# Filler transposes ahead of a wait in the scan, and two ScalarE splits behind eight evacuations, in a two-layer decoder trunk

## The reference

```python
xr, xw, xk, xv, xa, xg = [xf + xx * mu[i] for i in range(6)]
r = xr @ wr;  k = xk @ wk;  v = xv @ wv
w_log = -softplus(-(w0 + tanh(xw @ w1) @ w2)) - 0.5
decay = exp(-exp(w_log))
a = sigmoid(a0 + (xa @ a1) @ a2)          # the "rate"
g = sigmoid(xg @ g1) @ g2                 # the gate
...
def step(S, inp):                         # over the 256 tokens, 16 heads of 64x64
    sa = einsum('bhij,bhj->bhi', S, -kk_t)
    S = S * w_t + sa[..., None] * (kk_t * a_t) + v_t[..., None] * k_t
    y = einsum('bhij,bhj->bhi', S, r_t)
```

## Time and profile before

| | us |
|---|---|
| three runs | 1564.68, 1568.73, 1569.08 |
| median of the runs | 1568.73 |
| the profiled execution | 1557.25 |
| its span | 1555.2 |
| TensorE busy | 1521.9 (98%) |
| VectorE busy | 1264.2 (81%) |
| ScalarE busy | 997.4 (64%) |

### The profile page before, as it was taken

How to read it: one execution, slowest core, us unless ns; L and a number is a source line. 1 busy time by engine, 2 the same in 40 slices (tenths; PEclk the granted TensorE clock), 3 DMA queues, 4 the chain that set the end, 5 groups by cost and what they waited for, 6 DMA issues and landing times.

```text
span 1555.2 us, 21510 instructions
## 1 busy us (share of the span) xinstructions
PE 1521.9 (98%) x7832; PEld 1257.1 (81%) x7832; DVE 1264.2 (81%) x1449; ACT 997.4 (64%) x1139; POOL 9.3 (1%) x10
## 2 busy tenths in 40 slices
PE   8999999899999999999999999999999999999997
PEld 5678888589889767888888888888888888888885
DVE  3456666866866259999999999999999999999997
ACT  2244444553422138887887887878888888887886
POOL 0000000000000010000000000000000000000000
PEclk9999999999999999999999999999999999999999
DMA  9779443024003649999999999999999999999970
GB/s 362 286 277 300 163 162 109 0 82 140 22 1 110 227 176 400 397 377 363 387 366 358 387 361 359 385 381 343 383 381 344 381 379 349 376 379 357 370 292 27
DMA packets 203269, 439.36 MB, mean 283 GB/s; under 512 B 7217, under 2 KB 44337, under 8 KB 203090
## 3 DMA queue, kind: packets, MB, share of 16 engines
q1 hardware_dynamic: 200434, 434.05, 76.4%
q10 hardware_dynamic: 2208, 2.50, 0.5%
q0 software_dynamic: 576, 2.10, 0.3%
HBM read 427.09 MB, written 11.53 MB: 282 GB/s over the span
## 4 chain that ended last, share of the span: by engine, by line
PE 94%; DVE 3%; ACT 1%; issue 1%; DMA 0%; DVEq 0%; ACTq 0%
PE psum L1494 19%; PE psum L1496 19%; PE psum L1495 19%; PE psum L567 6%; PE psum L2227 5%; PE psum L2229 3%; PE psum L2155 2%; PE psum L842 2%; PE psum L2200 2%; PE psum L1512 2%; PE psum L2211 1%; PE psum L2213 1%; PE psum L2212 1%; PE psum L738 1%; PE psum L728 1%; PE psum L643 1%
## 5 line engine op out<-in xcount | busy, mean ns | idle before, releaser
L1694 DVE TENSOR_TENSOR w_lo<-ring,w_hi 128x1024 fp32r<-128x1024 f32 x672 | 805.0, 1221 | 51.5 <-ACT w_hi L1598 11.4
L1598 ACT ACTIVATE w_hi<-ring 128x1024 fp32r<-128x1024 f32 x672 | 711.4, 1062 | 186.6 <-PE psum L1496 186.4
L1494 PE MATMUL psum<-w_hi,xg_split 128*128 128x512 f32 x896 | 353.5, 395 | 0.4 <-DVE xg_split L1788 0.4
L1496 PE MATMUL psum<-w_lo,xg_split 128*128 128x512 f32 x896 | 349.4, 390 | 0.0
L1495 PE MATMUL psum<-w_hi,xg_split 128*128 128x512 f32 x896 | 348.8, 389 | 0.0
L1496 PEld LDWEIGHTS psum<-w_lo,xg_split 128*128 128x128 f32 x896 | 168.2, 188 | 35.7
L1494 PEld LDWEIGHTS psum<-w_hi,xg_split 128*128 128x128 f32 x896 | 168.2, 188 | 34.1 <-DVE xg_split L1788 0.6
L1495 PEld LDWEIGHTS psum<-w_hi,xg_split 128*128 128x128 f32 x896 | 168.4, 188 | 33.6
L1494 PE MATMUL psum<-w_hi,ht_split 128*128 128x512 f32 x448 | 176.0, 393 | 1.7 <-DVE w_lo L1694 1.7
L1496 PE MATMUL psum<-w_lo,ht_split 128*128 128x512 f32 x448 | 174.5, 390 | 0.0
L1495 PE MATMUL psum<-w_hi,ht_split 128*128 128x512 f32 x448 | 174.3, 389 | 0.0
(11 more groups left out here) (332 smaller groups left out, 1558.4 us busy)
## 6 DMA issues: line engine op xcount, KB each, us to landing
ring<-o_moe_wg_dram SPq DMA_DIRECT2D x56, 2048.0 KB, 9.1
ring<-o_moe_wu_dram SPq DMA_DIRECT2D x56, 2048.0 KB, 9.2
ring<-o_moe_wd_dram SPq DMA_DIRECT2D x56, 2048.0 KB, 9.1
ring<-e_ffn_wg_dram SPq DMA_DIRECT2D x11, 1024.0 KB, 5.5
ring<-e_ffn_wu_dram SPq DMA_DIRECT2D x11, 1024.0 KB, 8.7
ring<-e_ffn_wd_dram SPq DMA_DIRECT2D x11, 1024.0 KB, 10.6
expert_rows<-work SPq DMA_DIRECT2D x1, 8192.0 KB, 29.4
ring<-e_w_in_dram SPq DMA_DIRECT2D x2, 2048.0 KB, 18.1
```

Of the source, the lines that this page charges most:

```text
L1494: nc.tensor.matmul(dst, x_hi, hi, start=first, stop=False)
L1496: return nc.tensor.matmul(dst, x_hi, lo, start=False, stop=last_)
L1598: nc.scalar.activation(w_hi[:, (4 * i + n) % 4, :], piece(i, n), ACT.Copy).then_inc(m_hi, 1)
L1694: V.tensor_tensor(w_lo[:, r, :], piece(i, n), w_hi[:, r, :].bitcast(F32), ALU.subtract).then_inc(m_lo, 1)
```

## The change

Two edits, both of order only. No instruction is added or taken away, and no wait is added or taken away.

```diff
-            pe.wait_ge(y_zero, 3)
             pe.wait_ge(a_ma, 16)
             for _ in range(22):
                 nc.tensor.transpose(psum[:, 2, 0:P], ident, ident)
+            pe.wait_ge(y_zero, 3)
```

```diff
                 i_.then_inc(o_act, 1)
-                if n == 7:
-                    hi_x(0)
-                    hi_w(2)
+            hi_x(0)
+            hi_w(2)
             hi_x(1)
             hi_w(3)
```

## The result

Five executions of the changed kernel took 1552.04 us in the median (1550.95 to 1559.89). Five of the kernel before on the same chip took 1564.68 us (1564.31 to 1569.08). The ratio is 0.9916, with a 95% interval of 0.989 to 0.9942: 12.6 us less, where 5.8 were forecast. (Some 4 us of the distance to 1562.9 is only that these five runs of before have a median of 1564.68, the first three one of 1568.73.)

A forecast was written before the change was run, and what follows sets the result against it. TensorE's work and the gaps in it were taken to bound the kernel; 4.8 us (fillers) + 1.0 us (splits) = 5.8 us off the profiled 1557.25, ratio 0.9963, so 1568.73 became 1562.9 us, range 1557.5 to 1569.

The forecast's parts named there:

- the sum: Whole kernel: 4.8 + 1.0 = 5.8 us off the profiled 1557.25, giving 1551.45; same ratio 0.9963 on the median, 1562.9.
- part 2: Time mixing, two splits moved behind the rate's evacuations: TensorE's 1.00 us wait before the gate's first product goes, gaining 1.0 us.
- The bounds I gave: For the moved splits: at best the 1.0 us gap, at worst -1.0 us if lo_x(0)'s 2.0 us delay came through.
- Part 1's term: Scan, 22 fillers run inside the memset wait instead of behind it: L719 starts 4.75 us earlier; 4.8 us taken, bounds 4.2 to 5.0.
- The wait left: Sign in the scan: TensorE's 3.78 us wait shrinks to about 1.1 us and stands at L719.
- L1238 has lost its idle time: Sign in the scan: VectorE's first mask, L1238, no longer has 4.30 us of idle time before it, but none.
- Rivals A: Scan: the clock falls in the gap left ahead of L719; gain only 3.3 us, time 1565.4; chance 0.10.
- D: Scan from 433 on: clock falls behind the early fillers and isn't brought back; slower, 1574.9 us; chance 0.05.
- Rivals B: Time mixing: the moved splits gain nothing, another wait takes the gap's place; gain 4.8 us, time 1563.9; chance 0.07.
- C: Expert stage: ends where it did because the weight stream sets its pace; no gain, 1568.7 us; chance 0.11.
- TensorE's wait for L938 is gone: Sign at the gate's first product: this wait disappears and L592 starts 1.0 us earlier, at about 317.8.

The follow-up runs named there:

- the copy: The kernel before, run again unchanged: 1568.05 us in the median, ratio 1.0003; its profiled execution took 1568.47 us.
- part 2 alone: Kernel before with only hi_x(0) and hi_w(2) moved behind the rate's eight evacuations, the wait ahead of the fillers as before: 1556.68 us, ratio 0.9953.
- part 1 alone: Kernel before with only the wait for the memsets moved behind the 22 fillers, the splits where they were: 1566.23 us, ratio 0.9993.
- experiment 9: Part 1 alone plus 6 more transposes in the router's last two gaps (four ahead of its last rows, 12 for 10 behind): 1560.25 us, ratio 0.9969.
- experiments 5: Kernel before, orders kept, with 9 filler transposes behind the last rate product, in TensorE's 1.0 us gap: 1558.01 us, ratio 0.9947.

## Why the prediction was wrong

**The step that failed** is in the sum: "The runs' median is 11.48 us above the profiled execution. I take the same ratio for it: 1568.73 x 0.9963 = 1562.9." It took the profiled execution for a typical one, shorter only by chance. The runs show that it belongs to a group of 7 in 89. In its profile the clock does not fall at 309; in the copy's it does, and the missing 11 us stand right behind the very gap that part 2 closes. I had the 11.48 us in the text and explained it with nothing. Nearly twice the whole forecast, it called for a cause before a ratio.

**Part 2's term was mis-sized by that.** Its own gap is worth 1.08 us in the profiles and 0.8 us between free executions (forecast 1.0). What it mostly prevents is worth far more: free executions go from 7 of 89 (4 of 40 on the same chip) to 7 of 10 with part 2 alone. The bounds I gave, -1.0 to 1.0 us, were worked out from waits only. The clock was never asked about there, though it was for the other gap.

**Part 1's term was right.** From part 2 alone to both, free executions go from 1556.55 to 1551.9: 4.7 us (forecast 4.8). That it agrees to a tenth is partly luck: in the one profile of part 2 alone the clock fell later in the scan and for 3.4 us only, and its fillers held L719 back by 4.13 us and not 4.75. The wait left is 0.97 us (forecast 1.1), the fillers last 2.62 us (2.6), L1238 has lost its idle time, and the clock at the fillers stays at 1.00.

**The sum for one free execution was right.** 1557.3 to 1551.9 is 5.4 us and the profiles give 5.9 (forecast 5.8), and 1551.9 is close to what the sum had for the profiled execution (1551.45). The median of before fell by another 7 us because of the falls it mostly carried.

**The rule that I set aside.** The Trainium skill, "TensorE: Matmul & The Clock Gate", section "A second HAM failure mode: psum-queue depth-cycling", says that small idle moments between groups of matmuls can make the clock swing. I weighed it for the gap at L719, on the ground that a gap of 1.42 us elsewhere showed a clock of 1.00. For that place it held: all seven profiles that have this gap (0.97 to 0.98 us) show a clock of 1.00 there. Rivals A and D did not come true. For the 1.00 us ahead of the gate's products the row misled: one execution with the clock up doesn't show that a gap is harmless. There a short idle moment did bring a fall, which is nearer to the page, though it speaks of frequent ones in another kernel and here a single one of 1.00 us was enough. In the stretch of the 1.42 us gap, too, the clock fell in another execution, the second profile of the changed kernel, 1.7 us behind that gap and 0.2 us behind the next one, of 0.46 us:

```profile
286.00:287.00 1.00, 0.54 (x3) 0.29 (x3) 1.00 (x3) 0.98 (x2) 0.00 (x0) 0.87 0.00 0
287.00:290.00 3.00, 3.00 (x9) 1.36 (x8) 2.93 (x9) 0.69 (x1) 0.00 (x0) 0.50 0.00 0
```

**Rivals B and C** are refuted. TensorE's wait for L938 is gone and nothing came in its place, and the gain reaches the end: from the first expert product to the end of the span it is 977.9 us in the profile of before, 978.0 in its copy and 978.1 in the changed kernel's second profile. C's mechanism, a gain lost on the way, did occur in part 1 alone, but through the clock at 576 and at the very end, and not through the weight stream.

## What to carry to other kernels

- Where the timed median stands further from the profiled execution than the change is worth, profile several executions before forecasting. The mean granted clock of each tells at once whether they differ by it.
- Price a gap on TensorE by what runs behind it, not by its length. A gap of 1.0 us went with a loss of 11 us here, because the work behind it ran at half clock for 24 us.
- Fillers that fit into a wait cost nothing and kept the clock; behind the wait they cost their full length, doubled by the fallen clock.

## What the runs showed of the hardware

- TensorE busy without a break is no assurance of its clock. In the copy of before it fell at 308.94 and stayed at 1.2 GHz through all of the gate's products and 5.4 us of L592, 23.9 us in all. In one execution of the changed kernel it fell inside the gate's products at 315.84, with no gap near. In each of these it rose some 5 to 6 us into L592.
- The times of the kernel before come in distinct groups 3 to 4 us apart (1557.3, 1561.6, 1564.3, 1568.7), not in one spread. In the copy of before (1568.47 us) the gate's products took 18.47 us, in experiment 9's profile, where the fall came later, 16.06, and in the changed kernel's first profile the fall came later still and lost 4.9 us. That suggests that the groups go with how late the early fall comes. It is not shown: of the kernel before only executions of the first and the last group were profiled.
- Falls in different places may be tied. The late fall at 565 to 583 showed in part 1 alone, with the gap restored, without fillers, and in the changed kernel's execution at 1559.89. Each of these had a fall at the gate's products or in the scan as well. But such a fall was not enough: the kernel before, its copy, part 2 alone and experiments 5 and 9 had one and no late fall. What ties them was not settled. No run here varies the moment of a fall while it leaves the gaps alone.
- The clock can fall in the last products too. In six of the fourteen profiles it did so among TensorE's last eight, which take 0.39 us each at 2.4 GHz and 0.63 us at 1.2; from the first of them to the end it is then up to 0.8 us more.
